# Two decoder blocks in split fp32: high weights against high and low activations in one 512-column matmul

## The reference, cut to what matters

```
h = rmsnorm(x) ; proj = h @ w_in                       # first block: xr, yr, q, k, v, gates
xr = conv4(xr) ; rg_lru(xr) ; y_rnn = xr * gelu(yr)     # gates of the LRU by small block matmuls
y_att = window attention with sinks(rope(q), rope(k), v)
mix = sig(g_rnn) * (y_rnn @ w_rnn_proj) + sig(g_attn) * (y_att @ w_attn_proj)
x += rmsnorm(mix @ w_out)
x += rmsnorm(relu(rmsnorm(x) @ w_mlp_up)**2 @ w_mlp_down)
# second block: three kinds of attention (dilated "A", "B", compressed and selected "C"), w_out_2,
x += attention(rmsnorm(x) @ w_in_2) @ w_out_2
a, v = conv3(rmsnorm(x) @ w_up_2) split in two ; x += (silu(v) * a) @ w_down_2 ; x = rmsnorm(x)
```

## Time and profile before

| | |
|---|---|
| median of 3 runs | 3195.14 us (3194.42 to 3196.63) |
| profiled execution, span | 3192.2 us |
| PE busy | 2921.2 us, 92% |
| DVE busy | 1830.6 us, 57% |
| ACT busy | 1337.3 us, 42% |
| loaded from HBM | 491.90 MB, 157 GB/s over the span |

### The profile page before, as it was taken

How to read it: one execution, slowest core, us unless ns; L and a number is a source line. 1 busy time by engine, 2 the same in 40 slices (tenths; PEclk the granted TensorE clock), 3 DMA queues, 4 the chain that set the end, 5 groups by cost and what they waited for, 6 DMA issues and landing times.

```text
span 3192.2 us, 63492 instructions
## 1 busy us (share of the span) xinstructions
PE 2921.2 (92%) x23110; PEld 2828.7 (89%) x23110; DVE 1830.6 (57%) x2946; ACT 1337.3 (42%) x2144; POOL 155.2 (5%) x220
## 2 busy tenths in 40 slices
PE   5553989999999899999999969999989999999997
PEld 4553989888999799999999959989879999999997
DVE  6321876555555666545664463464567776477754
ACT  4223444444444444333443333454454443444443
POOL 1000020000000200000000020000010000000000
PEclk9776999999999899999999988999999999999999
DMA  4653435333555355555555533434335555555554
GB/s 137 125 117 80 171 134 174 129 132 132 175 180 184 119 184 182 186 184 173 182 184 184 184 122 130 158 109 152 117 117 190 179 179 173 193 183 179 180 168 144
DMA packets 92739, 503.42 MB, mean 158 GB/s; under 512 B 15867, under 2 KB 24347, under 8 KB 41435
## 3 DMA queue, kind: packets, MB, share of 16 engines
q1 hardware_dynamic: 84044, 491.63, 44.9%
q0 software_dynamic: 8624, 10.84, 2.7%
HBM read 491.90 MB, written 10.49 MB: 157 GB/s over the span
## 4 chain that ended last, share of the span: by engine, by line
PE 84%; DMA 7%; DVE 4%; issue 2%; ACT 1%; DVEq 0%; POOL 0%; SPq 0%; ACTq 0%; POOLq 0%
PE PS L529 25%; PE PS L531 25%; PE PS L530 25%; DMA w_raw<-in_w_X 4%; DMA bias_rows<-rows 1%; DVE w_lo L1520 1%; PE PS L593 1%; PE PS L595 1%; PE PS L594 1%; DMA w_raw<-in_w_RG 1%; PE PS L733 1%; ACT w_hi L954 1%; PE PS L756 1%; PE PS L679 1%; PE PS L748 1%
## 5 line engine op out<-in xcount | busy, mean ns | idle before, releaser
L1520 DVE TENSOR_TENSOR w_lo<-w_raw,w_hi 128x1024 fp32r<-128x1024 f32 (+3 forms) x1020 | 1106.0, 1120 | 625.4 <-ACT w_hi L954 624.9
L954 ACT ACTIVATE w_hi<-w_raw 128x1024 fp32r<-128x1024 f32 (+3 forms) x1020 | 956.1, 966 | 662.8 <-PE PS L531 298.8
L529 PE MATMUL PS<-h_hi,w_hi 128*128 128x256 f32 x3264 | 958.6, 294 | 126.6 <-DVE w_lo L1520 100.3
L530 PE MATMUL PS<-h_lo,w_hi 128*128 128x256 f32 x3264 | 935.1, 286 | 0.0
L531 PE MATMUL PS<-h_hi,w_lo 128*128 128x256 f32 x3264 | 934.3, 286 | 0.0
L529 PEld LDWEIGHTS PS<-h_hi,w_hi 128*128 128x128 f32 x3264 | 636.2, 195 | 171.8 <-DVE w_lo L1520 103.5
L530 PEld LDWEIGHTS PS<-h_lo,w_hi 128*128 128x128 f32 x3264 | 638.5, 196 | 0.5
L531 PEld LDWEIGHTS PS<-h_hi,w_lo 128*128 128x128 f32 x3264 | 637.8, 195 | 0.0
L529 PE MATMUL PS<-u_hi,w_hi 128*128 128x256 f32 x1728 | 489.9, 284 | 3.7 <-DVE w_lo L1520 3.7
L530 PE MATMUL PS<-u_lo,w_hi 128*128 128x256 f32 x1728 | 489.8, 283 | 0.0
L531 PE MATMUL PS<-u_hi,w_lo 128*128 128x256 f32 x1728 | 489.7, 283 | 0.0
(11 more groups left out here) (262 smaller groups left out, 2854.8 us busy)
## 6 DMA issues: line engine op xcount, KB each, us to landing
w_raw<-in_w_FU SPq DMA_DIRECT2D x88, 1024.0 KB, 4.8
w_raw<-in_w_UP SPq DMA_DIRECT2D x64, 1024.0 KB, 4.7
w_raw<-in_w_DN SPq DMA_DIRECT2D x64, 1024.0 KB, 4.8
w_raw<-in_w_FD SPq DMA_DIRECT2D x64, 704.0 KB, 4.1
w_raw<-in_w_G SPq DMA_DIRECT2D x32, 1024.0 KB, 4.8
w_raw<-in_w_Q SPq DMA_DIRECT2D x18, 1024.0 KB, 4.8
w_raw<-in_w_X SPq DMA_DIRECT2D x16, 1024.0 KB, 21.1
w_raw<-in_w_Y SPq DMA_DIRECT2D x16, 1024.0 KB, 4.8
```

Source lines behind the costliest of these rows:

```text
L529: pe.matmul(acc, w0, r0, start=start and k == 0, stop=False)
L530: pe.matmul(acc, w0, r1, start=False, stop=False)
L954: act.activation(w_hi[:, 2 * s + hf, 0:n * P], w_raw[:, s, off * P:(off + n) * P], ACT.Copy)\
L1520: tt(w_lo[:, slot, 0:n * P], w_raw[:, s, off * P:(off + n) * P], w_hi[:, slot, 0:n * P].bitcast(F32), ALU.subtract).then_inc(lo_ready, 1)
```

## The change

High and low activations of a k-step now lie side by side (`h2`, `d2`, `u2`, `f2`, `oc2` with shape [128, chunks, 2, 256] in place of separate tensors), and so do high and low weights (`w2`). A k-step has two matmuls: the high weights with 512 columns (high activations, then low) fill a whole PSUM bank, and the low weights with the 256 high columns are added to its second half. The finished product is the sum of the two halves of the bank, which is made on eviction:

- by `merge`, a TENSOR_REDUCE on DVE over the pair of halves (X, Y, G, MR, MA, O, UP, DN0, C2, B2, A2);
- by a copy of one half on ACT and an addition on DVE (Q: `rope_in` and `join_q`; FU: `low_copy` and `conv`);
- by two additions into the accumulator (DN1, FD).

Stages RG, V, VC, VAB, OC, OA and OB keep three matmuls. Where ACT evicted (X, Y, G, O, C2, B2, A2), DVE now does. In Y, MA and UP the operation that writes the low part of a unit's result (`y_part`, `mix_part`, `up_part`) is moved behind the merge of the next unit.

```
-            def half_unit(u, s, hf, n, acc, rhs, k0, start, stop, ready=None):
+            def half_unit(u, s, hf, n, bank, rhs, k0, start, stop, ready=None, wide=True):
...
-                    pe.matmul(acc, w0, r0, start=start and k == 0, stop=False)
-                    pe.matmul(acc, w0, r1, start=False, stop=False)
-                    mm = pe.matmul(acc, w1, r0, start=False, stop=stop and k == n - 1)
+                    r = rhs[:, k0 + k]
+                    last = stop and k == n - 1
+                    if wide:
+                        pe.matmul(PS[:, bank, :], w0, r.rearrange("p a b -> p (a b)"), start=start and k == 0, stop=False)
+                        mm = pe.matmul(PS[:, bank, S:2 * S], w1, r[:, 0, :], start=False, stop=last)
...
+            def merge(out, s):
+
+                return dve.tensor_reduce(out, PS[:, s, :].rearrange("p (a b) -> p b a", a=2), AX.X, ALU.add)
...
@@ Q, ACT and DVE @@
-                act.activation(tmp[s][:, 0:S], PS[:, s, 0:S], ACT.Copy).then_inc(acc_free, 1)
+                act.activation(tmp[s][:, 0:S], PS[:, s, S:2 * S], ACT.Copy).then_inc(low_ready, 1)
+            def join_q(c, s):
+                dve.wait_ge(low_ready, c + 1)
+                tt(tmp[s][:, 0:S], PS[:, s, 0:S], tmp[s][:, 0:S], ALU.add).then_inc(acc_free, 1)
@@ Y, DVE @@
-                    dve.wait_ge(acc_free, 2 + T0["Y"] + c + 1)
+                    dve.wait_ge(half_done, units_done(U0["Y"] + c))
+                    merge(tmp[s][:, 0:S], s).then_inc(acc_free, 1)
+                    if not isinstance(i, int) or i + s:
+                        y_part(c - 1, 1 - s)
+                    dve.wait_ge(gelu_ready, c + 1)
                     tt(y, t2, tmp[s][:, 0:S], ALU.mult).then_inc(yr_ready, 1)
-                    dve.wait_ge(y_hi, c + 1)
-                    tt(d_lo[:, c, :], y, d_hi[:, c, :].bitcast(F32), ALU.subtract).then_inc(y_lo, 1)
@@ MA, DVE @@
-                    tt(tmp[2][:, 0:S], PS[:, s, 0:S], tmp[s][:, 0:S], ALU.mult).then_inc(acc_free, 1)
+                    link(merge(tmp[2][:, 0:S], s))
+                    tt(tmp[2][:, 0:S], tmp[2][:, 0:S], tmp[s][:, 0:S], ALU.mult).then_inc(acc_free, 1)
+                    if not isinstance(i, int) or i + s:
+                        mix_part(c - 1, 1 - s)
                     dve.wait_ge(acc_free, 2 + T0["MA"] + c + 1)
                     tt(tmp[4 + s][:, 0:S], tmp[2][:, 0:S], gates[:, c, :], ALU.add).then_inc(mix_ready, 1)
@@ UP, DVE @@
-                        stt(tmp[s][:, 0:S], PS[:, s, 0:S], 0.0, rstd, ALU.max, ALU.mult).then_inc(acc_free, 1)
+                        merge(tmp[s][:, 0:S], s).then_inc(acc_free, 1)
+                        if not isinstance(i, int) or i + s:
+                            up_part(c - 1, 1 - s)
                         dve.wait_ge(acc_free, 2 + T0[name] + c + 1)
+                        link(stt(tmp[s][:, 0:S], tmp[s][:, 0:S], 0.0, rstd, ALU.max, ALU.mult))
                         tt(tmp[4 + s][:, 0:S], tmp[s][:, 0:S], tmp[s][:, 0:S], ALU.mult).then_inc(relu_ready, 1)
@@ FU, ACT and DVE @@
+                def low_copy(i, s):
+                    act.wait_ge(half_done, units_done(U0[name] + 2 * i + s))
+                    act.wait_ge(acc_free, T0[name] + 2 * i + s + 1)
+                    act.activation(low[:, s, :], PS[:, s, S:2 * S], ACT.Copy).then_inc(low_ready, 1)
...
-                    dve.wait_ge(half_done, units_done(U0[name] + 2 * i + s))
-                    tt(tmp[s][:, 2:2 + S], PS[:, s, 0:S], rstd2[:], ALU.mult).then_inc(acc_free, 1)
+                    dve.wait_ge(low_ready, 18 + 2 * n_v + 2 * i + s + 1)
+                    tt(tmp[s][:, 2:2 + S], PS[:, s, 0:S], low[:, s, :], ALU.add).then_inc(acc_free, 1)
                     dve.wait_ge(acc_free, 2 + T0[name] + 2 * i + s + 1)
+                    link(tt(tmp[s][:, 2:2 + S], tmp[s][:, 2:2 + S], rstd2[:], ALU.mult))
```

More of the change, by code:

```diff
@@ L193, in program @@
         k2s, kcs = tmp[0:3], tmp[3]
+        low = place("low", [P, 2, S], at=reg_k + 3 * KB)
         sinks = place("sinks", [P, 32])
@@ L1317, in tile_c @@
                     copy_step(JOB_C, t, e, copy_c)
-                    act.wait_ge(half_done, units_done(U0["A2"] + k))
-                    act.activation(qk2[:, k, :], PS[:, e, 0:S], ACT.Copy).then_inc(acc_free, 1)
                     if more:
                         exp_step(JOB_C, t + 1, e, exp_c)
-            with act.Fori(0, 4) as i:
-                project("B2", i, 12)
+            splits("B2", 4)
             exp_step(JOB_C, 0, 0, exp_c)
@@ L1656, in body @@
                         rope(c - 1, 1 - s, qy[:, c - 1, :])
+                    join_q(c, s)
             link.begin(0, 5 + 3 + 2)
@@ L1669, in _ @@
             rope(15, 1, qy[:, 15, :])
+            join_q(16, 0)
             next_lo(U0["Q"] // 2 + 8, 1, SUB)
@@ L1746, in body, with mix_part @@
                     dve.wait_ge(half_done, units_done(U0["MR"] + c))
-                    tt(gates[:, c, :], PS[:, s, 0:S], tmp[s][:, 0:S], ALU.mult).then_inc(acc_free, 1)
-            run_pairs(dve, "MR", 8, body)
+                    dve.wait_ge(acc_free, T0["MR"] + c + 1)
+                    link(merge(tmp[2 + s][:, 0:S], s))
+                    tt(gates[:, c, :], tmp[2 + s][:, 0:S], tmp[s][:, 0:S], ALU.mult).then_inc(acc_free, 1)
+            run_pairs(dve, "MR", 8, body, link=link, per=2)
+            def mix_part(c, s):
+                dve.wait_ge(mix_hi, c + 1)
+                tt(d_lo[:, c, :], tmp[4 + s][:, 0:S], d_hi[:, c, :].bitcast(F32), ALU.subtract).then_inc(mix_lo, 1)
             def body(i, n):
@@ L1807, in splits, with project @@
                 run_pairs(dve, name, pairs_of[name], body)
-            splits("C2")
+            def project(name, i, s, n, out):
+                next_lo(U0[name] // 2 + i, s, n)
+                dve.wait_ge(half_done, units_done(U0[name] + 2 * i + s))
+                merge(out, s).then_inc(acc_free, 1)
+            with dve.Fori(0, 4) as i:
+                for s in range(2):
+                    project("C2", i, s, SUB, qk2[:, bass.ds(20 + 2 * i + s, 1), :].rearrange("p a b -> p (a b)"))
+            project("C2", 4, 0, SUB, qk2[:, 28, :])
+            for c in range(9, 12):
+                project("C2", c // 2, c % 2, SUB, tmp[(4, 5, 0)[c - 9]][:, 0:S])
             splits("VC")
@@ L2010, in body @@
                         dve.wait_ge(half_done, units_done(unit))
+                        if units == 2:
+                            link(tt(x[:, c, :], PS[:, s, S:2 * S], x[:, c, :], ALU.add))
                         tt(x[:, c, :], PS[:, s, 0:S], x[:, c, :], ALU.add).then_inc(acc_free, 1)
-                run_pairs(dve, name, 8, body, peel=gain is not None)
+                run_pairs(dve, name, 8, body, peel=gain is not None, link=link if units == 2 else None, per=2)
                 if gain:
@@ L2059, in body @@
                     conv(i, 1).then_inc(av_ready, 1)
-                run_pairs(dve, name, FF2_H, body, peel=True, link=link, per=4)
+                run_pairs(dve, name, FF2_H, body, peel=True, link=link, per=6)
                 gated(FF2_H - 1)
```

204 lines of the change are left out of this document (110 added, 94 removed).

## The result

| | runs, median us (lowest to highest) | ratio to before, 95% interval |
|---|---|---|
| before | 3195.4 (3194.4 to 3196.6), 4 runs | |
| after | 3164.1 (3155.7 to 3169.1), 4 runs | 0.9901 [0.9887, 0.9914] |
| forecast | 3111, range 3070 to 3190 | 0.974 |

The change makes the kernel 1% faster: 31 us, where 84 were forecast. The profiled execution has a span of 3164.1 us, 28.1 less than before.

A forecast was written before the change was run, and what follows sets the result against it. PE was taken to pace nearly all stages. PE-paced stages and FD -78.3, FU -17.6, Q -3.7, UP +2.6, MA +3.0, Y +5.7, X and RG +2, ends +2.5 sum to -83.8 off 3195.1: 3111 us, range 3070 to 3190.

The forecast's parts named there:

- the pace of the k-step, 0.336: Two-matmul k-steps on PE: wide 0.216 plus short 0.120 us, where three matmuls took 0.36; a 16-step unit 5.38.
- A cost added to each matmul should not vanish at the lower clock: PE's short matmul: 0.21 us at low clock taken to mean something beside the stream sets 0.12, hidden beside 512 columns.
- rival 1: PE: the 13 ns are a cost of each matmul; k-step 0.347, unit 5.55, total 3147 us; chance 0.19.
- The merge at 0.68: DVE's TENSOR_REDUCE over the two halves of the bank takes 0.68 us, bounds 0.42 and 1.2.
- rival 3: UP, MA and Y: merge of 1.2 in place of 0.68 makes the rings worse, +48, total 3159 us; chance 0.09.
- The ring becomes 5.8: UP: DVE and ACT taking turns on eviction and weight split set the pace at 5.8 us a unit, +2.6 in all.
- PE waits for w_lo at each unit: Sign expected in UP and MA: PE waits for the low weights each unit, with units of 5.8 and 5.95 us.
- Y at 6.2: Stage Y: merge, handover and gelu lengthen the step between evictions from 5.02 to 6.2 us a unit, +5.7 in all.
- FU's bound at DVE's sum, 5.56: Stage FU: an added tensor_tensor brings DVE's work to 5.56 us a unit, above PE's 5.38; -17.6 over 88 units.
- Q at 5.97, by DVE's sum: Stage Q: DVE's work including join_q sets 5.97 us a unit, where it was 6.19; -3.7 in all.
- X and RG, and the ends: Extra work behind slow transfers in X and RG, +2 us; merge delaying last evictions at eight stage ends, +2.5.
- Half of the k-steps' gain never shows: Whole kernel: of 162 us gained by 6752 k-steps, half stays hidden as UP, MA, Y, FU, Q turn to DVE and ACT.

The follow-up runs named there:

- e1_micro: PE alone, none of the reference's work: stretches of fp32r matmuls of several widths and weight sizes; 256 columns took 120.0 ns, 384 173.3, 512 226.7.
- e8_pace2: Changed kernel with the short matmul cut from 256 to 208 columns, so part of the low-weight term is missing; 3122.6 us, ratio 0.9773.
- e4_order: Changed kernel with ACT's rounding of a unit's result moved behind its split of the weights in Y, MA and UP; 3149.8 us, ratio 0.9853.
- e2_grouped: Changed kernel with all wide matmuls of each half unit first, then all short ones, in place of taking turns; 3157.8 us, ratio 0.9893.
- e3_three: Changed kernel with three matmuls of 256 columns per k-step again, new evictions and order kept; 3212.9 us, ratio 1.0054.

## Why the prediction was wrong

**The step that failed: the pace of the k-step, 0.336.** I split the 0.12 of a short matmul into 0.107 of stream and 13 ns that must be hidden beside 512 columns, because at the low clock the same matmul takes 0.21, which leaves nothing over. "A cost added to each matmul should not vanish at the lower clock": it does. e1_micro shows the 13.3 at three widths, 512 among them: a wide matmul takes 0.227 by itself, not 0.216. The low clock was one observation, and I read it as excluding a mechanism. All it shows is what happens at that clock (the changed kernel's short matmul is again 0.21 there). Why the cost is absent there was not tried. That L748's records take 0.22 each was not evidence either: 512 columns and 13.3 ns are 0.227, and 0.22 lies between the two. The Trainium skill (TensorE: Matmul & The Clock Gate, "Back-to-back issue gap") has 2.5 ns for what is 13.3 here.

With that alone rival 1 would have come: k-step 0.347, and 3147. The remaining 17 us are mostly a thing that none of my cases had: the second pattern, 0.353, in which most stages run. Its 0.1 us a unit is worth 16 us in the stages that PE paces (148 units without C2) and 8 in FU; the rings of UP and MA, shorter than I had them, give part of it back, and the clock in V and VC takes 4.

By stages, change of length in us in the profiled executions (from the first matmul of a stage to the first of the next; FD1 to its last k-step). The stages "paced by PE" are G, MR, O, DN, C2, B2 and A2:

| | forecast | after | e8_pace2 (k-step 0.340) |
|---|---|---|---|
| paced by PE | -61.4 | -18.4 | -45.1 |
| FD | -16.9 | -5.0 | -10.4 |
| UP | +2.6 | -5.1 | -5.9 |
| MA | +3.0 | -1.7 | -2.5 |
| Y | +5.7 | +8.1 | +8.0 |
| FU | -17.6 | -8.6 | -17.5 |
| Q | -3.7 | -2.9 | -4.8 |
| X, RG | +2.0 | +0.8 | +1.6 |
| ends and the rest | +2.5 | +4.6 | +4.9 |
| sum | -83.8 | -28.1 | -71.8 |

**The other steps.**
- The merge at 0.68: right (0.686), and rival 3 with it out.
- "The ring becomes 5.8" in UP and 5.95 in MA: the ring is there (no idle time before the merge), and in e8_pace2 it sets the pace, but it is 5.68 in both stages and both kernels. At PE's real 5.65 it did not count in the changed kernel, and the sign "PE waits for w_lo at each unit" did not come. The working was off by itself too: 4.77 and 0.99 are 5.76 and not 5.8, so the whole +2.6 for UP was rounding, and 4.99 and 0.93 are 5.92. In the rows of UP1, L1822 starts 1.39 after the merge (1564.75 - 1563.36) where I had 1.45, which leaves 5.70; in MA it is 1.39 for my 1.5, which leaves 5.81, and the rest down to 5.68 I can't assign to one operation.
- Y at 6.2: right (6.24 and 6.36 in turn), +8.1 for +5.7. The merge lengthens the ring, and the order on ACT puts it in PE's way: with the same merge and e4_order's order the unit is 5.55.
- FU's bound at DVE's sum, 5.56: right as a bound (5.53 and 5.58 in e8_pace2), but at 5.65 PE came first, so it gave half.
- Q at 5.97, by DVE's sum: 5.99 came, but by luck. It is PE's 16 k-steps of 0.3467 and 0.44 for the rotation, and it followed PE down to 5.88 in e8_pace2, below the bound that I had.
- X and RG, and the ends: the +4.6 that came for +2.5 is mostly not a delayed eviction but the clock, which I had at nothing: V +2.5 and VC +1.6. e2_grouped has the same merges, the clock of before in both, and neither is longer. Why the clock fell in V in one kernel and not in the other is not settled: PE had waited in Y before it in both. e3_three's +19 for all that the evictions cost is near my 15.8, but of other parts: UP and MA gave 0.8 of my 5.6, and V and VC 4.1.
- "Half of the k-steps' gain never shows": 6752 k-steps at 0.353 and 0.347 gave some 50 us (e3_three less the changed kernel), and the evictions took 20 of it back. With the pace right, the sum would have been right within a few us by the estimate from e8_pace2, but partly by luck: I had UP and MA 14 us too long, and Y, the ends and the stages paced by PE too short.

## What to carry to other kernels

When a pitch is made of a stream and something else, measure it at two lengths and two sizes of the weights before you sum thousands of them: one row at another clock could not tell which part is hidden. A wider matmul saves the cost of the instructions that it removes (13.3 ns each here) and nothing of the columns, so 6752 fewer matmuls save PE at most 90 us here (6752 x 13.3 ns, an estimate). Where two engines take turns, put the operation that only a later stage needs behind the one that the next unit waits for: that was worth 11.5 us in Y here, over a third of what the change itself gave. And before a longer stage is put down to work in it, look at the granted clock of that stage alone: V's 2.5 us stood in no digit of the 40 slices.
